# One odd mixer's front in another order, and the key spread in other matmuls (macaron model of two layers, one core)

## The reference

```
def layer(x, i):
    x = x + 0.5 * swiglu(rms_norm(x, ffn1_norm[i]), ...)
    x = x + (even_mixer if i % 2 == 0 else odd_mixer)(rms_norm(x, mix_norm[i]), ...)
    return x + 0.5 * swiglu(rms_norm(x, ffn2_norm[i]), ...)

def odd_mixer(h, ...):
    glu, q, k, v, qi, ki, wi = _split(h @ w_in, ODD_SPLITS)
    ca, cg = jnp.split(glu, 2, axis=-1)
    c = causal_depthwise_conv(ca * jax.nn.sigmoid(cg), dw_w, dw_b)      # 31 taps
    c = jax.nn.silu(layer_norm(c, ln_g, ln_b))
    q, k = head_rms(q), head_rms(k)
    yd = dsa_attention(q, k, v, qi, ki, wi, rel_bias)
    return jnp.concatenate([c, yd], axis=-1) @ w_out

# in dsa_attention, for each query: which 128 keys it may look at
    sc = relu(qi . ki)                             # 8 index heads of width 64
    isc = sum over heads of sc * wi, causal
    sel = top_k(isc, 128)
    p = softmax(q . k[sel] / 8 + rel_bias[rel_bucket(t - sel)])
```

## Time and profile before

| | before |
|---|---|
| median of 3 runs (lowest to highest) | 2090.51 us (2086.25 to 2090.68) |
| the profiled execution | 2090.39 us |
| its span, first to last instruction | 2088.6 us |
| PE busy | 97% |
| DVE busy | 52% |
| mean granted TensorE clock (1 is 2.4 GHz) | 0.979 |

### The profile page before, as it was taken

One profiled execution on the slowest core, in us unless ns is written; L12 is line 12 of the kernel. 1 busy time (PEld: TensorE's weight loads), 2 busy tenths in 40 slices (PEclk: granted clock), 3 DMA queues, 4 the chain that ended last, 5 costly groups with the idle time before them and its releaser, 6 DMA issues.

```text
span 2088.6 us, 25069 instructions
## 1 busy us (share of the span) xinstructions
PE 2018.0 (97%) x8902; PEld 1643.5 (79%) x8902; DVE 1094.1 (52%) x1688; ACT 780.1 (37%) x1117; POOL 49.6 (2%) x87
## 2 busy tenths in 40 slices
PE   7999999999889999999999999989799899999999
PEld 5888888877768888888888888867668678888887
DVE  5443445666664444446444344628977654443435
ACT  4222223476653223224322222443356653222222
POOL 1000000000000000000000000010100000000000
PEclk9999999999999999999999999998999899999999
DMA  4263333211112222223232223474644253233232
GB/s 166 96 130 116 131 101 103 99 61 51 51 61 91 100 92 99 96 95 116 96 96 95 100 91 100 123 164 100 144 102 120 61 139 103 91 101 99 92 101 101
DMA packets 60574, 212.74 MB, mean 102 GB/s; under 512 B 6584, under 2 KB 6840, under 8 KB 60504
## 3 DMA queue, kind: packets, MB, share of 16 engines
q1 hardware_dynamic: 51936, 184.44, 26.8%
q0 software_dynamic: 6048, 22.02, 5.6%
q10 hardware_dynamic: 2520, 5.36, 1.4%
HBM read 184.79 MB, written 4.72 MB: 91 GB/s over the span
## 4 chain that ended last, share of the span: by engine, by line
PE 88%; DVE 5%; ACT 4%; issue 2%; DMA 0%; SPq 0%; ACTq 0%; DVEq 0%
PE ps_unit L500 27%; PE ps_unit L502 27%; PE ps_unit L501 27%; PE ps_s L500 1%; PE ps_misc L590 1%; DVE top L1557 1%; DVE isc L1561 1%; PE ps_t L625 1%; PE ps_y L500 1%; PE ps_s L502 1%; PE ps_y L502 1%; PE ps_y L501 1%; PE ps_s L501 1%; ACT L962 0%; ACT w_hi L855 0%
## 5 line engine op out<-in xcount | busy, mean ns | idle before, releaser
L500 PE MATMUL ps_unit<-xs_hi,w_hi 128*128 128x512 f32 x1768 | 703.4, 398 | 16.4 <-DVE xs_lo L1191 11.0
L855 ACT ACTIVATE w_hi<-raw 128x1024 fp32r<-128x1024 f32 x301 | 319.2, 1061 | 1038.5 <-PE ps_unit L502 1021.9
L501 PE MATMUL ps_unit<-xs_lo,w_hi 128*128 128x512 f32 x1768 | 693.4, 392 | 0.0
L502 PE MATMUL ps_unit<-xs_hi,w_lo 128*128 128x512 f32 x1696 | 663.8, 391 | 0.0
L1183 DVE TENSOR_TENSOR w_lo<-raw,w_hi 128x1024 fp32r<-128x1024 f32 x301 | 368.2, 1223 | 85.0 <-ACT w_hi L855 84.7
L500 PEld LDWEIGHTS ps_unit<-xs_hi,w_hi 128*128 128x128 f32 x1768 | 335.3, 190 | 97.2 <-issue 11.2
L501 PEld LDWEIGHTS ps_unit<-xs_lo,w_hi 128*128 128x128 f32 x1768 | 335.3, 190 | 71.9 <-issue 3.4
L502 PEld LDWEIGHTS ps_unit<-xs_hi,w_lo 128*128 128x128 f32 x1696 | 320.9, 189 | 67.9
L500 PE MATMUL ps_unit<-a_hi,w_hi 128*128 128x512 f32 x884 | 350.6, 397 | 11.7 <-DVE a_lo L1442 4.3
L501 PE MATMUL ps_unit<-a_lo,w_hi 128*128 128x512 f32 x884 | 347.8, 393 | 0.0
L502 PE MATMUL ps_unit<-a_hi,w_lo 128*128 128x512 f32 x846 | 331.3, 392 | 0.0
(11 more groups left out here) (211 smaller groups left out, 1358.2 us busy)
## 6 DMA issues: line engine op xcount, KB each, us to landing
raw<-w_stream_dram SPq DMA_DIRECT2D x343, 512.0 KB, 3.4
w_lo<-raw POOLq DMA_DIRECT2D x28, 512.0 KB, 5.0
w_lo_3rd<-raw POOLq DMA_DIRECT2D x14, 512.0 KB, 4.9
skew<-table ACTq DMA_DIRECT2D x1, 2560.0 KB
bias_t<-skew ACTq DMA_DIRECT2D x1, 2048.0 KB, 9.4
out_dram<-xt SPq DMA_DIRECT2D x8, 256.0 KB, 2.0
xt<-xt_in_dram SPq DMA_DIRECT2D x7, 256.0 KB, 5.9
bd_raw<-bd_in_dram SPq DMA_DIRECT2D x1, 512.0 KB, 8.1
```

Source lines behind the costliest of these rows:

```text
L500: pe.matmul(ps, lhs_hi, rhs_hi, start=first, stop=False)
L501: pe.matmul(ps, lhs_hi, rhs_lo, start=False, stop=False)
L502: return pe.matmul(ps, lhs_lo, rhs_hi, start=False, stop=last)
L855: act.activation(w_hi[:, s, :], raw[:, slot, :], ACT.Copy).then_inc(w_hi_done, 1)
```

## The change

In the odd mixer two gated units (m = 0, 1) now stand ahead of the five index units. The 24 index rows stand inside the units m = 2 to 7, one behind each quarter of a unit (`ROWS_AFTER`), not six behind a whole one. On DVE a round or a tap follows each row; taps no longer stand inside rounds. Of the 48 rounds, 16 lie with the gated units, 10 with the two conv units that are left there, 22 in all five slots of the first pair, which now has two conv units of its own in slots 3 and 4 (those of j = 1). 15 taps moved to the index units, and the second and third pair have 41 taps where they had 28. In both mixers `spread_k` is now four matmuls of 128 columns against the identity, each with its own weights, for two of 512 columns with fixed ones; DVE makes one copy for them, not two products. In the even mixer the first gate product of slot 1 stands in the middle of that slot's unit, and DVE's `lru_low` ahead of `k_normed`.

```diff
-TAPS_AFTER = ((2, 3, 3, 4, 4), (3, 3, 3, 3, 2), (3, 3, 3, 3, 2))
+GLU_FIRST = 2
+ROWS_AFTER = {2: (0, 0, 1, 1), 3: (1, 1, 1, 1), 4: (1, 1, 1, 1), 5: (1, 1, 1, 1), 6: (1, 1, 1, 2), 7: (1, 1, 1, 2)}
+FIRST_ROW = {m: sum(sum(ROWS_AFTER[k]) for k in range(2, m)) for m in ROWS_AFTER}
+IDX_TAPS = (3, 3, 3, 3, 3)
+ROW_TAPS = {4: 2}
+ROW_ROUNDS = {4: 2, 5: 4, 6: 5, 7: 5}
+CONV_ROUNDS = (5, 5)
+PAIR_ROUNDS = (5, 4, 4, 4, 5)
+PAIR_TAPS = ((1, 1, 0, 0, 0), (4, 4, 4, 4, 4), (5, 4, 4, 4, 4))
...
-ODD_IN = [3, 3 + CONV_UNITS, 3 + CONV_UNITS, 3]
+ODD_IN = [3 + CONV_UNITS, 3 + CONV_UNITS, 3 + CONV_UNITS, 3]
...
-                pe.matmul(ps_misc[:, :], head_row[:, HD:3 * HD], diag[:, :], start=True, stop=False)
-                pe.matmul(ps_misc[:, :], head_row[:, 0:2 * HD], acc[:, :], start=False, stop=True).then_inc(kbc_done, 1)
+                for t in range(TT):
+                    b = slice(t * P, (t + 1) * P)
+                    mm = pe.matmul(ps_misc[:, b], diag[:, b], ident[:, :], start=True, stop=True)
+                mm.then_inc(kbc_done, 1)
...
+                        elif it and u == 1:
+                            start_unit(n)
+                            blocks(n % 2, range(KT // 2), of_x(1), of_x(0))
+                            lru_gate(it - 1, 0)
+                            blocks(n % 2, range(KT // 2, KT), of_x(1), of_x(0)).then_inc(unit_done, 1)
...
+                for m in range(GLU_FIRST, GLU_IN):
+                    n, q = n0 + IDX_IN + m, FIRST_ROW[m]
+                    start_unit(n)
+                    for part, rows in enumerate(ROWS_AFTER[m]):
+                        mm = blocks(n % 2, (2 * part, 2 * part + 1), of_x(1), of_x(0))
+                        if part == 3:
+                            mm.then_inc(unit_done, 1)
+                        for _ in range(rows):
                             index_row(q)
...
+                            q += 1
+                for c in range(CONV_UNITS):
+                    conv_unit(0, c, n0 + IDX_IN + GLU_IN + c)
...
-                for h in range(2):
-                    inv = hinv[:, a % 2, 2 * TT:].rearrange("p (t h) -> p t h", h=2)[:, :, h]
-                    ins = dve.tensor_tensor(blocks_of((diag, acc)[h][:, :]), ident_4, column_4(inv), ALU.mult)
-                ins.then_inc(kdiag_done, 1)
+                inv = hinv[:, a % 2, 2 * TT:].rearrange("p (c o) -> p c o", o=1).to_broadcast([P, 2 * TT, HD])
+                dve.tensor_copy(diag[:, :].rearrange("p (c f) -> p c f", f=HD), inv).then_inc(kdiag_done, 1)
...
-                    k_normed(a)
                     if 0 < a < 4:
                         lru_low(a - 1)
+                    k_normed(a)
...
-                if c % 3 == 0:
-                    tap()
...
+                    for q in range(FIRST_ROW[m], FIRST_ROW[m] + rows):
+                        index_row(q)
+                        if taps_left:
+                            tap()
+                            taps_left -= 1
+                        elif rounds_left:
+                            cut_round(rounds)
+                            rounds, rounds_left = rounds + 1, rounds_left - 1
+                    for _ in range(taps_left):
+                        tap()
+                    glu_in(m, n)
...
+                        if it == 0 and u < len(PAIR_ROUNDS):
+                            for _ in range(PAIR_ROUNDS[u]):
+                                cut_round(rounds)
+                                rounds += 1
...
-                            for c in range(TAPS_AFTER[it][u]):
+                            for _ in range(PAIR_TAPS[it][u]):
                                 tap()
```

More of the change, by code:

```diff
@@ L1634, in odd @@
                     dve.memset(c_pad[j][:, 0:DW_TAPS - 1], 0.0).then_inc(pad_done, 1)
[L1635 to L1637 removed]
+                for m in range(GLU_FIRST):
+                    n = n0 + m
+                    if m == 0:
                         split_lo(n + 2, (n + 2) % RAW, (n + 2) % 2)
@@ L1641, in odd @@
                         dve.wait_ge(half_done, i + 1)
+                    glu_in(m, n)
+                    if m:
+                        split_lo(n + 2, (n + 2) % RAW, (n + 2) % 2)
+                        glu(m)
+                for u in range(IDX_IN):
+                    n = n0 + GLU_FIRST + u
                     dve.wait_ge(unit_done, n + 1)
+                    if u == 1:
+                        dve.wait_ge(glu_done, 1)
                     if u >= 2:
@@ new lines, in odd @@
+                    for _ in range(IDX_TAPS[u]):
+                        tap()
+                dve.wait_ge(wi_turned, 1)
+                w = ps_misc[:, :].rearrange("p (t f) -> p t f", f=P)[:, :, HD:HD + HEADS]
+                dve.tensor_scalar(wi.rearrange("p (t h) -> p t h", h=HEADS), w, (HD ** -0.5) * (HEADS ** -0.5), None,
+                                  ALU.mult).then_inc(wi_done, 1)
+                dve.wait_ge(wi_done, 1)
+                rounds = 0
+                for m in range(GLU_FIRST, GLU_IN):
+                    n, rows = n0 + IDX_IN + m, sum(ROWS_AFTER[m])
+                    taps_left, rounds_left = ROW_TAPS.get(m, 0), ROW_ROUNDS.get(m, 0)
+                    for q in range(FIRST_ROW[m], FIRST_ROW[m] + rows):
+                        index_row(q)
+                        if taps_left:
[5 more added lines that the diff above has]
+                    for _ in range(taps_left):
+                        tap()
+                    glu_in(m, n)
+                    split_lo(n + 2, (n + 2) % RAW, (n + 2) % 2)
+                    if m % 2:
+                        glu(m)
+                    if m == 4:
+                        conv_low(1)
+                    for _ in range(rounds_left):
+                        cut_round(rounds)
+                        rounds += 1
@@ L1695, in odd @@
                             split_lo(n + 2, (n + 2) % RAW, (n + 2) % 2)
-                        if it == 0 and u == 0:
-                            for c in range(44, 48):
-                                cut_round(c)
+                        if it == 0 and u < len(PAIR_ROUNDS):
+                            for _ in range(PAIR_ROUNDS[u]):
+                                cut_round(rounds)
+                                rounds += 1
                         if it == 3 and u == 1:
@@ L1791, in lay_out @@
     kiwi[:, :HD + HEADS] = odd[:, 3072:3072 + HD + HEADS]
+    units += pair(odd, (0, 512), 0)
     units.append(columns(kiwi, 0, 1))
     units.append(columns(odd, 2560, 4))
-    for i in range(4):
+    for i in range(1, 4):
         units += pair(odd, (0, 512), i)
-    for i in range(2):
-        units += tap_units(a["od_dw_w"][0], i)
+    units += tap_units(a["od_dw_w"][0], 0)
     for i in range(4):
```

118 lines of the change are left out of this document (49 added, 69 removed).

## The result

| | before | after |
|---|---|---|
| median of 5 runs each (lowest to highest) | 2090.51 us (2086.25 to 2091.94) | 2068.05 us (2063.92 to 2073.07) |
| the profiled execution, and its span | 2090.39, 2088.6 us | 2068.05, 2066.3 us |
| PE busy; DVE busy | 97%; 52% | 97%; 53% |
| mean granted TensorE clock | 0.979 | 0.986 |

The account below looks back on a forecast made before the run. PE, busy 97%, was taken as the bound, with DVE deciding where dense in the odd mixer. 24.6 - 3.1 + 1.6 + 5.8 = 28.9 us off 2090.39 gave 2061.5, stated as 2061, range 2050 to 2074.

Parts of the forecast that it names:

- front to the first score: Odd mixer up to the first score: the first score starts at 1505.0 instead of 1529.63, giving back 24.6 us.
- 13 later taps: Second and third pair of the odd mixer: 10.1 us more DVE work, mostly in idle time; 3.1 us lost.
- spread behind the first score: Odd mixer's second and third pair: each spread takes 0.9 us instead of 1.7, saving 1.6 us in all.
- even mixer: Gate product 4.1 us back, `lru_low` 0.65 saved but 1.3 lost, spread 0.8, clock 1.5: 5.8 us.
- The rows: 24 index rows inside units m = 2 to 7: 15.7 us of PE time, bounds 12.2 and 19.
- PE's way: Odd mixer's front: six gated units (32.6) with the rows (15.7) bring PE's first conv unit to about 1449.1 us.
- DVE from there on: From the first conv unit, DVE's rounds and other operations sum to 55.9 us and set the first score at 1505.0.
- PE's waits: PE waits some 14 us for DVE: about 2 ahead of `head_ssq`, 8 for `v_lo`, 4 for `k_lo`.
- the later taps land on the path: Rival, chance 0.15: second and third pair pay the taps' 10.1 us in full, 7 more than forecast; 2068 us.
- The sign of being wrong: Prediction is wrong if the slots of the second and third pair grow by more than 3 us together.
- the rows did not wait inside the units: Rival, chance 0.13: rows wait inside the units for late relus, 0.5 us for each of 22 rows, costing 11; 2072.
- this rival: Slower, chance 0.04: TensorE at 1.2 GHz through m = 2 to 7, PE work there 41 us longer; 2102 us.

Follow-up runs that it names:

- the kernel with `v_lo` first: Changed kernel with the first pair's `v_lo` ahead of slot 3's four selection rounds instead of behind them; 2068.12 us in one execution.
- the one with fewer rounds: Changed kernel with 4 of the last query tile's 16 selection rounds left out; 2063.44 us in one execution.

## Why the prediction came out as it did

2061 was forecast, with 2050 to 2074; it is 2068.05. The mechanisms were the ones named, and three terms were mis-sized. The three errors go one way, 6.5 us together; the range held them.

| term of the sum | predicted | measured |
|---|---|---|
| front to the first score | 24.6 | 20.6 |
| 13 later taps | -3.1 | -5.1 |
| spread behind the first score | 1.6 | 1.1 |
| even mixer | 5.8 | 6.3 |
| span | 28.9 | 22.3 |

(The last row of the measured column also holds the 0.5 us that the start took longer; -5.1 is the -4.1 of the stretches behind the first score without the 1.1 of the spread.)

*The rows* are the step that failed: "with about 0.15 a row for leaving and re-entering a unit I take 15.7; the upper bound is 19". They cost 20.3 (53.0 less six units of 5.44), beyond the bound. A row takes 0.21 us more than its columns (0.55, 0.72 and 0.87 to 0.89 against 0.34, 0.51 and 0.68), and the blocks behind it 0.23 more, 0.44 together and not 0.15, at 22 places (24 times 0.15 on the lower bound would have been 15.8, not 15.7). Against that two rows together cost one, which the prediction had not either. The experiment with rows two at a time confirms both: 12 places of 0.44 and the columns of 12 rows come to 11.4, and the six units took 44.0 - 32.6 = 11.4.

*PE's way*: so the first conv unit ended at 1447.9 and, the mixer having begun 5.8 us earlier (1347.49 against 1353.29), this is 4.6 later than the 1449.1 of the prediction. *DVE from there on*: 55.9 us predicted, 55.3 measured (1447.9 to 1503.2). This chain, built from durations of single operations of before, was right to 1%, and the kernel with `v_lo` first shows that it is a sum, of which the order doesn't matter; the one with fewer rounds shows that it is so for the first 4 us only. The copy in it took 0.43, not 0.7. PE's waits, foretold as 2, 8 and 4, were 1.6, 5.5 and 1.6, together 5 us less. Not because PE came later to the conv units, since DVE starts from there too, but because PE's own way from the first conv unit to the first score took 55.3 - 8.7 = 46.6 us, and the prediction's terms for it come to 41 (it says 42): it was reckoned at full clock, and the first pair ran at 0.90. As foretold, the lowered clock cost nothing there, since DVE decides.

*The taps*: of the three places named, the turn in the third pair waits 1.0 us (0.9 was foretold) and the sum for the layer norm 2.6 (1.4). The turn in the second pair, priced at 0.8, does not wait; a later one there does, for 0.2. So the places were right in two of three and the size was not: 13 taps left out save 4.1 to 6.7, 4.1 of it waits. The rival "the later taps land on the path" had 10.1, so the truth lies between, by the waits nearer to the forecast. That the 2.7 us of clock belong to the taps isn't shown. The sign of being wrong, a growth of the second and third pair by more than 3 us together, was just missed: they grew by 2.7, with the cheaper spread in them.

*The spread*: the saving of 0.8 was right (the four small matmuls take 0.81, eight records of 0.101), but that it counts once in the even mixer is only argued: the waits for `pt_lo` and `a_lo` give back 2.5 of 3.2 us, and the 0.7 that should stay were not seen. DVE was behind at more places than I had looked at.

*The even mixer*: 4.1 for the gate product is measured on both sides. `lru_low` saved its 0.65, and `k_lo` cost 1.0 and not 1.3. The 1.5 for the clock can't be told from chance, since the same instructions differ by 4 to 5 us between executions, so that the sum came out at 6.3 against 5.8 is partly luck.

*The rivals*: the rows did not wait inside the units (no relu wait is left in the list). Nor did the clock fall among them: 22 groups of small products in two changing banks, between blocks of a unit, ran at 1.00. The page that I had set beside this rival, of the Trainium skill (TensorE: Matmul & The Clock Gate, A second HAM failure mode: psum-queue depth-cycling), speaks of idle times between groups; here PE had none, so the trace neither confirms nor refutes it.

## What to carry to other kernels

Price small products put inside a large one by place and not by instruction. Here each place cost 0.44 us on top of the columns of one row of three matmuls, whether one or two such rows with 64 channels stood there, the two on different halves of the array. The chain on the engine that decides could be added up from single operations to 1%, and once it is added up, ask of every member by when it is really needed: five selection rounds stood there that nobody needed for two more slots. Work moved to "idle time" in late slots cost 0.3 to 0.5 us for an operation of 0.78, and nothing only where the engine's idle time lies ahead of no one who waits.

## What the runs showed of the hardware that I had not expected

- Two products with 64 channels each on different halves of the array's rows run together: two rows of 512 keys 0.90 us, one 0.87 to 0.89; two of 384 keys 0.73, one 0.72; two of 256 0.56, one 0.55. The Trainium skill (TensorE: Matmul & The Clock Gate, Why this matters for your kernels) says of small-K matmuls that those on distinct row groups run concurrently. The trace agrees.
- DVE's copy of 512 fp32 columns took 0.43 us, the product with two operands 0.69 (the same 128 x 512 tile, L1345 and L1344). The Trainium skill (VectorE: DVE Perf Modes, The perf-mode tier table) gives fp32 `tensor_copy` its 2x mode and `tensor_tensor` only 1x. The trace agrees in direction.
- The same instructions of the even mixer took 242.7 to 246.6 us in nine executions, with the mean clock 0.97 to 0.95; those of before took 252.8 at 0.95 and 247.7 at 0.97. That is nearly as much as the even mixer's whole edit brings (5.0 to 6.3).
